# Expert stages of a two-model kernel: two experts known beforehand, a fifteenth weight slot, the crowded branch at the second round, places ordered by TensorE

## The reference, cut to what matters

```python
def moe(h2, router_w, router_b, w1, w3, w2):          # h2: 256 x 1024
    scores = sigmoid(h2 @ router_w)                    # 16 experts in 4 groups of 4
    biased = (scores + router_b).reshape(256, 4, 4)
    gidx = argmax(sum(top_k(biased, 2)))               # the best group of a token
    _, loc = top_k(biased[gidx], 2)                    # its two best experts
    gates = sel / sum(sel)
    ...                                                # tokens sorted by expert
    y = (silu(xb @ w1[e]) * (xb @ w3[e])) @ w2[e]      # w1, w3: 1024 x 512, w2: 512 x 1024
    return sum of y * gate over a token's two experts
```

## Time and profile before

| | |
|---|---|
| median of 3 runs | 1951.69 us (1950.99 to 1953.96) |
| the profiled execution | 1957.06 us, span 1955.3 us |
| TensorE matmuls busy | 1749.1 us, 89% |
| VectorE, ScalarE, GpSimd busy | 964.8, 644.1, 94.8 us |
| moved by DMA | 430.10 MB, mean 220 GB/s |
| first expert stage | about 226 to 473 us of the span |
| second expert stage | about 608 to 867 us of the span |

### The profile page before, as it was taken

One profiled execution on the slowest core, in us unless ns is written; L12 is line 12 of the kernel. 1 busy time (PEld: TensorE's weight loads), 2 busy tenths in 40 slices (PEclk: granted clock), 3 DMA queues, 4 the chain that ended last, 5 costly groups with the idle time before them and its releaser, 6 DMA issues.

```text
span 1955.3 us, 23433 instructions
## 1 busy us (share of the span) xinstructions
PE 1749.1 (89%) x9480; PEld 1210.7 (62%) x9480; DVE 964.8 (49%) x1761; ACT 644.1 (33%) x1105; POOL 94.8 (5%) x136
## 2 busy tenths in 40 slices
PE   6998867998998679989989979999999798889997
PEld 5654633443676224447445658888887574679996
DVE  5673400002444000144577465887676846666665
ACT  2154121122232111132266445222232525654443
POOL 0790000000000000000000000000000100000000
PEclk8989989999999889999989989999999898989999
DMA  9978499999858999982200112445453121024530
GB/s 391 378 297 325 185 405 421 421 421 421 324 201 326 399 403 418 420 350 87 86 1 1 44 44 93 187 175 212 173 214 151 65 89 41 4 103 176 186 137 22
DMA packets 61863, 430.10 MB, mean 220 GB/s; under 512 B 6576, under 2 KB 9776, under 8 KB 9904
## 3 DMA queue, kind: packets, MB, share of 16 engines
q1 hardware_dynamic: 61744, 428.48, 54.9%
HBM read 427.40 MB, written 1.05 MB: 219 GB/s over the span
## 4 chain that ended last, share of the span: by engine, by line
PE 65%; DVE 15%; DMA 10%; ACT 7%; issue 2%; SPq 1%; DVEq 0%; ACTq 0%
PE bank L292 14%; PE bank L1100 11%; PE bank L296 10%; PE bank L298 9%; PE bank L297 9%; DMA ring<-in_ws_dram 7%; DMA work<-in_ws_dram 3%; DVE ring_halves L2421 2%; PE bank L331 2%; ACT work_halves L2415 2%; PE bank L2094 2%; PE bank L2071 2%; DVE work L438 1%; PE bank L2445 1%; DVE work L553 1%
## 5 line engine op out<-in xcount | busy, mean ns | idle before, releaser
L296 PE MATMUL bank<-work_halves 128*128 128x512 f32 (+1 forms) x1344 | 472.4, 351 | 29.0 <-DVE HH_halves L2713 15.1
L298 PE MATMUL bank<-work_halves,ring_halves 128*128 128x512 f32 (+1 forms) x1344 | 461.1, 343 | 0.0
L296 PEld LDWEIGHTS bank<-work_halves 128*128 128x128 f32 x1344 | 258.5, 192 | 66.4 <-DVE HH_halves L2713 16.2
L297 PE MATMUL bank<-HH_halves,work_halves 128*128 128x512 f32 (+1 forms) x832 | 289.3, 348 | 0.0
L1100 PE MATMUL bank<-ring,work 128*32 128x512 f32 (+2 forms) x896 | 257.7, 660 | 21.5 <-DMA work<-in_ws_dram 11.2
L298 PEld LDWEIGHTS bank<-work_halves,ring_halves 128*128 128x128 f32 x1344 | 258.4, 192 | 28.7
L1100 PE MATMUL bank<-work 128*32 128x512 f32 (+2 forms) x640 | 222.0, 640 | 35.8 <-DMA ring<-in_ws_dram 34.1
L2421 DVE TENSOR_TENSOR ring_halves<-ring,work_halves 128x2048 fp32r<-128x2048 f32 x72 | 164.7, 2287 | 51.0 <-ACT work_halves L2415 51.0
L297 PEld LDWEIGHTS bank<-HH_halves,work_halves 128*128 128x128 f32 x832 | 161.6, 194 | 20.5 <-issue 2.2
L297 PE MATMUL bank<-work_halves 128*128 128x512 f32 (+1 forms) x512 | 172.0, 336 | 0.0
L1378 DVE TENSOR_TENSOR work<-work,bank 128x512 f32<-128x512 f32 x14 | 9.6, 688 | 298.8 <-PE bank L1100 298.8
(11 more groups left out here) (339 smaller groups left out, 2291.0 us busy)
## 6 DMA issues: line engine op xcount, KB each, us to landing
ring<-in_ws_dram SPq DMA_DIRECT2D x287, 1024.0 KB, 10.3
work<-in_ws_dram SPq DMA_DIRECT2D x117, 1024.0 KB, 18.2
con<-in_con_dram SPq DMA_DIRECT2D x1, 1177.0 KB, 27.3
XX<-in_xT_dram SPq DMA_DIRECT2D x1, 1024.0 KB, 10.0
XX<-in_cT_dram SPq DMA_DIRECT2D x1, 1024.0 KB, 20.2
out_dram<-XX SPq DMA_DIRECT2D x2, 512.0 KB, 3.1
par<-in_par_dram SPq DMA_DIRECT2D x1, 338.0 KB, 2.9
con<-in_con_dram SPq DMA_DIRECT2D x1, 128.0 KB, 2.8
```

Of the source, the lines that this page charges most:

```text
L296: pe.matmul(out, l[0], r[0], start=start, stop=False)
L297: pe.matmul(out, l[0], r[1], start=False, stop=False)
L298: return pe.matmul(out, l[1], r[0], start=False, stop=stop)
```

## The change

- Expert 1 takes place 1 for sure: its key gets 2048 added, as expert 0's gets 4096. Now 12 loads of a stage are known beforehand. The other 14 experts take places 2 to 15 in order of count; by `RANK` the fullest of them has place 3.
- The rounds are now (1, 2), (8 to 11), (0), (4, 5), (3), (12 to 15), (6, 7), instead of (8 to 11), (0), (12 to 15), (1), (2, 3), (4, 5), (6, 7).
- A fifteenth slot, the half O1 of HH, joins the ring from the stage's fifth load until the fifth step. It is free when the mixer's output product has used it. A load into it is written in runs of 1 KB.
- The branch moves from before the first `pe_fill` to the start of step 1, on the three engines. The crowded code itself is rewritten for that spot (smaller loads, other buffers).
- TensorE orders positions and gates by place: four transposes of 16 columns, a copy by ScalarE, four small matmuls by the one-hot matrix `hot`. VectorE's wide products and sums go. The counts by place come from one more small matmul.
- `rank_below` becomes `rank_in_four`, with fewer instructions in a row.
- The picks move behind the four evictions of rows on VectorE. The load of ctx waits for a later group and is issued earlier in the plan.

```diff
-ROUNDS = ((8, 9, 10, 11), (0,), (12, 13, 14, 15), (1,), (2, 3), (4, 5), (6, 7))
+ROUNDS = ((1, 2), (8, 9, 10, 11), (0,), (4, 5), (3,), (12, 13, 14, 15), (6, 7))
+RANK = (0, 1, 3, 2) + tuple(range(4, 16))
+ROOM = tuple(next(CAP // len(r) for r in ROUNDS if p in r) for p in range(16))
...
+        ring.append(O1)
...
+                latest[WIDE + 1] = out.st, ("p", 3, 1)
+                slots.insert(4, WIDE + 1)
-                fixed = [key for key in self.w if key[2] == 0]
+                fixed = [key for key in self.w if key[2] < 2]
                 for key in fixed:
                     chunk(self.st, *key)
                     slots.pop()
-                for key in self.w:
+                for n, key in enumerate(self.w):
+                    if n == self.group[4][0].start:
+                        slots.remove(WIDE + 1)
                     if key in fixed:
                         slots.append(slot_of[key])
...
                 st.wait_ge(pe, "hot")
-                pe.matmul(bank[0][0:1, 0:16], con_("rows", ...), self.hot[0:16, :], ...)
-                for i in self.steps[1]:
-                    self.bg.pe(pe, i)
-                reg = self.load_count(pe)
-                with pe.If_lt(reg, CAP + 1):
-                    pe.drain()
-                with pe.Else():
-                    self.pe_more(pe)
-                self.after_more(pe)
+                pe.matmul(bank[0][0:1, 64:80], con_("rows", ...), hot, ...)
+                st.wait_ge(pe, "count")
+                pe.matmul(bank[3][0:1, 64:80], self.count[0:16, 0:1], hot, ...)
+                st.wait_ge(pe, "places")
+                for i, v in enumerate((self.pq, self.gate)):
+                    for a in range(2):
+                        c = 256 * i + P * a
+                        t = pe.transpose(bP[0:16, c:c + P], v[:, 16 * a:16 * a + 16], ident)
+                t.then_inc(st.pe("turned"), 1)
+                for i in self.steps[1][0:2]:
+                    self.bg.pe(pe, i)
+                st.wait_ge(pe, "turned at hand")
+                st.wait_ge(pe, "rows by count")
+                for i in range(4):
+                    t = pe.matmul(bank[0][:, 128 + 16 * i:144 + 16 * i], self.turned[:, P * i:P * i + P], hot, ...)
+                t.then_inc(st.pe("by place"), 1)
+                for i in self.steps[1][2:]:
+                    self.bg.pe(pe, i)
...
                 for e in range(NR + 1):
                     n = self.ahead(e)
+                    if e == 1:
+                        reg = self.load_count(pe)
+                        with pe.If_lt(reg, CAP + 1):
+                            pe.drain()
+                        with pe.Else():
+                            self.pe_more(pe)
+                        self.after_more(pe)
...
             def dve(self, dve):
-                self.pick(dve, 0)
-                self.pick(dve, 1)
                 for i in range(4):
                     ...                                  # evictions of rows
+                st.wait_ge(dve, "by place")
+                dve.tensor_copy(self.placed, bank[0][:, 128:192]).then_inc(st.dve("placed"), 1)
+                st.wait_ge(dve, "placed")
+                self.pick(dve, 0)
+                self.pick(dve, 1)
...
-        ctx_at = plan.index(("w1", 1, 4, 0))
+        ctx_at = plan.index(("w1", 1, 3, 0))
```

More of the change, by code:

```diff
@@ L45 @@
           ("cos64", 256), ("sin64", 256), ("cos32", 256), ("sin32", 256),
-          ("down", 16), ("place", 16), ("rows", 2)]
+          ("down", 16), ("rank", 16), ("short", 16), ("below", 1), ("rows", 2)]
 COFF = {}
@@ L1099, in pe_shared @@
                         c = slice(n * h, n * h + n)
-                        m = pe.matmul(b[c, :], left[:, k, c], ring_of(self.w[i])[:, 512 * k:512 * k + 512], start=first and k == 0, stop=last and k == 3,
+                        w = rows_of(self.w[i], k)
+                        m = pe.matmul(b[c, :] if slot_of[self.w[i]] <= WIDE else k8(b[c, :], 256), left[:, k, c], w, start=first and k == 0, stop=last and k == 3,
                                       skip_group_check=True)
@@ L1166, in pe @@
-                self.after_more(pe)
+                pe.matmul(bank[0][0:1, 64:80], con_("rows", slice(0, 16), self.l, self.l + 1), hot, start=True, stop=True).then_inc(st.pe("rows of weights"), 1)
+                st.wait_ge(pe, "count")
+                pe.matmul(bank[3][0:1, 64:80], self.count[0:16, 0:1], hot, start=True, stop=True).then_inc(st.pe("counts by place"), 1)
+                st.wait_ge(pe, "places")
+                for i, v in enumerate((self.pq, self.gate)):
+                    for a in range(2):
+                        c = 256 * i + P * a
+                        t = pe.transpose(bP[0:16, c:c + P], v[:, 16 * a:16 * a + 16], ident)
@@ L1201, in pe_more @@
                 x, a = self.more_x, k8(self.aT, CAP)
-                pm, pt = k8(self.Pm[1], CAP), self.PT[0]
-                for i in range(4):
-                    self.st.wait_ge(pe, "evicted", ("rows", i))
+                pm, pt = k8(self.more_pm, CAP), self.PT[1]
+                mask, down = self.mask, con_("down", slice(0, 1))
+                for key in (("w1", 0), ("w3", 0), ("spread", 0), ("fill", 1, 0, 0), ("fill", 1, 0, 1)):
+                    self.st.wait_ge(pe, "evicted", key)
+                mms(pe, bank[1][:, 0:16], [(ones, mask[:, 0:16]), (ones, mask[:, 16:32]), (ones[0:1, :], down)]).then_inc(st.pe("keys"), 1)
                 for u in range(32):
@@ L1233, in pe_more @@
-                    self.pe_scatter(pe, st, u, pt, False)
+                    bt = {n: bank_of(pe, st, ro, n, u) for n in ("w1", "w3")}
+                    for i, (name, j) in enumerate(EXPERT[0:4]):
+                        for h in range(2):
+                            n = 12 * u + 2 * i + h
+                            w = self.more_loaded(pe, n)
+                            st.wait_ge(pe, "evicted", ("gather", u, j))
+                            for k in range(2):
+                                t = pe.matmul(k8(bt[name][:, :], 128), x[:, 4 * j + 2 * h + k, :], w[:, 4 * k:4 * k + 4, :], start=j == h == k == 0, stop=j == h == k == 1)
+                            t.then_inc(st.pe("used", n), 1)
@@ L1339, in act_more @@
             def act_more(self, act):
-                st, ro = self.more, self.mo
-                order = [(n, self.l, u // 2, j) for u in range(32) for n, j in EXPERT]
+                st, ro, g = self.more, self.mo, self.g[1]
+                order = [(n, self.l, u // 2, j, h) for u in range(32) for n, j in EXPERT for h in range(2)]
                 def load(n):
@@ L1491, in order @@
[L1491 to L1501 removed]
+                st.wait_ge(dve, "rows of weights")
@@ L1502, in most_rows @@
+                dve.tensor_copy(cnt[0:1, 16:32], bank[0][0:1, 64:80]).then_inc(st.dve("rows by count"), 1)
+                most = self.most
+                st.wait_ge(dve, "counts by place")
+                dve.tensor_tensor(most[0:1, 0:16], bank[3][0:1, 64:80], con_("short", slice(0, 1)), ADD).then_inc(st.dve("raised"), 1)
                 st.wait_ge(dve, "raised")
-                dve.tensor_reduce(self.den[0:1, 0:1], self.c2[0:1, 48:64], AX.X, MAX).then_inc(st.dve("most"), 1)
+                dve.tensor_reduce(most[0:1, 16:17], most[0:1, 0:16], AX.X, MAX).then_inc(st.dve("most"), 1)
```

286 lines of the change are left out of this document (149 added, 137 removed).

## The result

| | before | changed |
|---|---|---|
| median | 1952.12 us (4 runs, 1950.99 to 1953.96) | 1968.81 us (4 runs, 1967.50 to 1972.27) |
| ratio to before | | 1.0085, 95% interval 1.0071 to 1.0099 |
| the profiled execution, span | 1957.06, 1955.3 us | 1972.27, 1970.5 us |

The change makes the kernel 16.7 us slower by the medians, and 15.2 us by the two profiled executions. The forecast was +5.8 us with a range up to 1967. The direction was right. The size was a third of what came, and the result lies just outside the range.

The account below looks back on a forecast made before the run. The prediction took DMA to set the end, with TensorE close behind. It added +3.6 us for the first stage and +2.2 for the second, together +5.8: 1951.7 + 5.8 = 1957.5 us, range 1945 to 1967.

Parts of the forecast that it names:

- The stream's rate and the head start: First stage: one 1 MB load per 2.49 us; without waits load 96 of 96 lands at 455.3, 10.7 us earlier.
- The price of a load that is issued shortly before the landing ahead of it: DMA queue: issued 4 us or more ahead costs nothing, 2.3 to 4 us 0.8, later 4.8 us from issue.
- Part 1, the slot O1: Fifteenth slot: load 5 lands at 228.7 us; each of two loads in 1 KB runs per stage costs 0.3 us.
- Part 2, a gain of nothing: Routing before the gather: earlier picks and evictions gain nothing, because the first group waits for load 13 at 249.9 us.
- Part 3, the branch: Jump of 6.4 us moves to the start of step 1; load 24 is 3.0 late, without the branch 0.6.
- The two rules on the jump: Price of the taken branch: 0.11 us by one, fetching a page by the other; the prediction followed the second, 6.4 us.
- Part 4, loads 16 to 36: First round of four, 7 slots: load 16 3.2 late, load 18 0.8, loads 28, 32 and 36 0.7 each.
- Part 4, loads 47, 67, 69 and 71: Steps 2, 3 and 4 of the first stage: these loads issued too shortly ahead, 3.3 us late together.
- The end of the stage: Last groups of four wait for w2, with a chance of a lower clock: nothing added, at most 1.8 us.
- The second stage: Second expert stage: same late list, but half of 4.3 us of existing small delays return, +2.2 us.
- Much slower: Middle rounds' late loads lose twice as much, lower-clock groups take 6.5 us: +5 to +8 more, 1964; chance 0.14.
- Faster: TensorE keeps its full clock, the jump is short, the head start lives: total 1938.4 us; chance 0.2.

Follow-up runs that it names:

- e8: The changed kernel with round (0) of known loads first, later rounds reordered, and the branch at step 3: 1948.3 us, ratio 0.9975.
- e1: The changed kernel with the branch moved back before the first gather on all three engines: 1959.3 us, ratio 1.0025.
- e5: The changed kernel with the branch and the crowded code left out on all three engines: 1959.1 us, ratio 1.0024.
- e6: The changed kernel with the old order of rounds behind (1, 2): 1968.6 us, ratio 1.0076.
- e2: The changed kernel without the fifteenth slot O1, so 14 slots: 1985.6 us, ratio 1.0172.
- e14: The changed kernel with round (0) moved from third to first place and the branch at step 3: 1949.4 us, ratio 0.9973.
- e7: The kernel before with only its branch moved, from before the first gather to the start of step 1: 1966.7 us, ratio 1.0074.
- e9: e8 with the branch before the first gather instead of at step 3: 1963.9 us, ratio 1.0043.
- e12: e8 with the branch at step 5 instead of step 3: 1947.3 us, ratio 0.9963.
- e10: The changed kernel with eleven 128x512 products added in two TensorE waits, seven before the first group and four later: 1967.2 us, ratio 1.0069.

## Why the prediction was wrong, point by point

The signs that the prediction named came true nearly all: the jump at step 1, the waits before the groups of four, the DMA gap, the last load at 470.4. What failed is the price of the jump.

- **The stream's rate and the head start** were right. Load 5 was put at 228.7 and came at 227.8 in an execution that ran 1.7 us ahead. Load 96 was put at 469.6 and came at 470.4; without those 1.7 us it would have been 2.5 off, so part of this nearness is luck.
- **The price of a load that is issued shortly before the landing ahead of it** was too small. Issued 2.1 us ahead, load 28 came 2.0 late (0.2 by the rule taken), and 3.3 ahead, load 32 of the second stage came 1.5 late (0.8). Loads issued 4.8 to 6.2 us ahead should have cost nothing; loads 22 and 34 of the first stage and 6, 22, 30 and 46 of the second came 1.2 to 1.4 late, about 8 us in all.
- **Part 1, the slot O1.** The price of 0.3 a load was too small: issued at 222.3 into an idle queue it took 5.6 us instead of 4.8, and the second load into it came 0.5 us late in each stage. The page counts 65445 packets instead of 61863, and four loads of 1024 packets instead of 128 are 3584 more.
- **Part 2, a gain of nothing** was right for the changed order, and for the reason given: load 13 covers it. But VectorE was 7 us earlier, not 3, so TensorE waited 6.8 us and not 3 to 4.7. The first two groups took 9.7 us, the first of them at a granted clock of 0.58. In e8 the round behind the gather needs no new load and starts at once; what the earlier gather alone is worth there was not measured.
- **Part 3, the branch. This is the step that failed.** The prediction had "3.0 late. Without the branch 0.6", so 2.4 us for a stage and 4.8 in all. The jump's length was right (6.4 put, 6.6 and 7.1 found), and so was its place. e1 and e5 put its price at 11.8 us, give or take some 3.5. Most of it is load 24 itself: 3.4 and 5.8 us late with the jump at step 1, nothing in e1, nothing and 0.4 in e5, so about 9 us where 4.8 was put. What the working left out is the clock behind the jump. It put the group there at 3.6 us, full clock, though its own rule adds 1.8 us to a group behind a wait over 2 us; by that rule the price would have been 8.4 us and the forecast 1961. The group took 5.0 us at a clock of 0.73 in the first stage and 6.6 at 0.55 in the second. The 2 to 3 us that remain are not pinned: load 16 comes less late in e1, but also in e6, where the jump has not moved, and loads 28 to 36 are as late in e1 as with the jump at step 1.
- **The two rules on the jump.** The figure of the Trainium skill, Advanced Engine Details and Errata, Control Flow Timing (about 0.11 us for a compare and a branch), would have made e1 and the changed kernel equal; they are 11.7 us apart. By the Trainium skill, Runtime: NRT & Kernel Launch, Instruction fetch mechanics, a taken branch outside the fetched window must first fetch its page. The trace agrees: the jump is idle time without a releaser, 6.3 to 10.7 us, wherever it is put, and between 269.1 and 275.7 us of the changed kernel three packets of instructions are moved, where e5 moves none in the same stretch:

```profile
q8 instruction: 1, 0.02, 1.0%
q14 instruction: 2, 0.02, 0.8%
```

- **Part 4, loads 16 to 36** were right in mechanism. Load 16 came 4.1 late (3.2 put), load 18 not at all (0.8 put); loads 28 to 36 with small ones between came 4.2 late (2.1 put). e2 confirms that slots are what these loads wait for.
- **Part 4, loads 47, 67, 69 and 71**, 3.3 late: they weren't late in either stage, but issued 4.3 to 10.2 us ahead. The working also lets step 2 free 14 slots; by the rounds as listed it is 12 (four of round (0) and eight w2 of the round of four). Why they had more room than was counted was not taken apart.
- **The end of the stage**, "I add nothing for it, at most 1.8": 2.7 us, and 0.9 in the work behind it, in the first stage. Of this e14 shows 1.8 by the order of the last rounds alone. The jump is not the cause: e1 and e5 end 8.7 and 9.1 us behind load 96. The rest is not pinned down.
- **The second stage**, +2.2: +7.0. Of the 4.8 that are missing, load 24 makes 2.8 (5.8 against 3.0).
- **Rivals.** "Much slower" had the sign and half of the cause (groups at the lower clock), but put the rest on the middle rounds, which lost nothing, and stopped at 1964. "Faster" needed load 24 issued 4 us ahead of load 23's landing; it was issued 1.1 and 3.5 us behind it.

By the terms: 5.8 forecast, 7.0 missing from the branch, 3.6 from the end of the first stage, and 16.4 of 16.7 is accounted for. That it closes so well is partly luck: the branch's price has its 3.5 us of uncertainty, and the smaller terms cancel, some 8 us too low for the loads issued 5 to 6 us ahead against 6.6 too high for loads 47 to 71 of both stages.

## What to carry to other kernels

- When a stage hangs on a ring of buffers, count late loads, not idle time: a stall of one engine costs what it makes late. One jump of 6.5 us cost nothing measurable in place of a wait, 6 us a stage where the ring was thin, and made no load late where loads were issued 14 to 25 us ahead. Look at what follows the stall: with groups of four behind it (the changed kernel) one load was late by it; with single groups, each of which frees one slot (e7, e9), up to five were.
- Knowing more loads beforehand helps if the work that uses them comes first. With the jump out of the way, the same two known experts were 0.24% slower than the kernel before with a first round that also needs an unknown expert (e5), and 0.25 to 0.37% faster with a first round that needs known ones alone (e8, e12, e14).
- Price a group behind a wait or a jump at the lower clock when the next slot hangs on it.

## What the runs showed of the hardware that was not expected

- The jump over the crowded code is not of fixed length: 6.3 to 7.1 us in most places, but 8.3 us in e9's first stage and 10.7 us in e10's second. Packets of instructions are moved within it.
- Added products of 128x512 in waits delayed nothing: the groups behind the seven and behind the four still waited 0.95 and 1.43 us for their loads in e10's first stage. The seven brought the granted clock of the next group from 0.58 to 1.00.
- Single loads came 1.0 to 1.6 us late, once 2.4, though they were issued 5 to 11 us ahead of the landing before them, one to four in most stages, at changing places. No slot that they waited for explains them, since they were issued that early; the cause is open.
